# Order of work in a two-block transformer kernel: MLA's fill and keys, neighbourhood scores, weight splits

## The reference

```python
def first_block(x, ...):                       # two layers
    h = rms_norm(x, g_mix[l])
    c_q, c_kv, k_r, qkv_b, qkv_c, gate_logits = split(h @ w_in[l])
    y_a = mla_mixer(c_q, c_kv, k_r, ...)       # 8 heads, latent queries, keys and values, full softmax
    y_b = dilated_mixer(q_b, k_b, v_b)         # 3 groups of 4 heads (dilation 1, 4, 16), banded
    y_c = neighbourhood_mixer(q_c, k_c, v_c, rpb[l])   # 8 heads, 8 x 16 window on a grid, bias
    merged = sum(sigmoid(gate_n) * (y_n @ w_pn[l]) for n in "abc")
    x = x + merged @ w_o[l]
    x = x + (silu(h2 @ w1[l]) * (h2 @ w3[l])) @ w2[l]

def second_block(x, ...):
    x = x + retention_mixer(rms_norm_2(x), ...)    # 4 heads of 256, rope, chunks of 128, decay
    x = x + swiglu_ffn(rms_norm_2(x), ...)
    x = x + rglru_mixer(rms_norm_2(x), ...)        # gelu branch * RG-LRU(conv4(u)), width 1536
    x = x + swiglu_ffn(rms_norm_2(x), ...)
```

## Time and profile before

| | |
|---|---|
| runs | 3466.03 us in the median (3464.95 to 3467.26) |
| the profiled execution | 3467.91 us, its span 3466.1 us |
| mean granted clock | 0.988 of full |
| TensorE matmul (PE) | busy 3376.0 us, 97% |
| VectorE (DVE) | busy 1796.0 us, 52% |
| ScalarE (ACT) | busy 1321.6 us, 38% |
| GpSimd (POOL) | busy 600.6 us, 17% |
| DMA | 86 GB/s in the mean, 25.5% of 16 engines |
| chain that ended last | PE 89%, DVE 6%, ACT 3%, POOL 1%, issue 1% |

### The profile page before, as it was taken

One profiled execution on the slowest core, in us unless ns is written; L12 is line 12 of the kernel. 1 busy time (PEld: TensorE's weight loads), 2 busy tenths in 40 slices (PEclk: granted clock), 3 DMA queues, 4 the chain that ended last, 5 costly groups with the idle time before them and its releaser, 6 DMA issues.

```text
span 3466.1 us, 38536 instructions
## 1 busy us (share of the span) xinstructions
PE 3376.0 (97%) x15644; PEld 2796.1 (81%) x15644; DVE 1796.0 (52%) x2674; ACT 1321.6 (38%) x2018; POOL 600.6 (17%) x518
## 2 busy tenths in 40 slices
PE   8899999999999899999999999999999999999998
PEld 7688778888888777778888878888888887788887
DVE  6755565544437554564444345554544347854433
ACT  4643453333225533543333223332333237843221
POOL 1321022011003320121111001120211014631101
PEclk9999999999999999999999999999999999999999
DMA  3012223222221111222222322222232222223322
GB/s 133 31 56 73 81 78 101 97 97 97 97 97 61 44 61 61 90 82 100 94 97 92 112 69 96 82 79 97 74 97 96 99 67 97 86 73 97 98 97 85
DMA packets 85425, 296.92 MB, mean 86 GB/s; under 512 B 9472, under 2 KB 11776, under 8 KB 85248
## 3 DMA queue, kind: packets, MB, share of 16 engines
q1 hardware_dynamic: 85248, 294.47, 25.5%
HBM read 292.33 MB, written 2.10 MB: 85 GB/s over the span
## 4 chain that ended last, share of the span: by engine, by line
PE 89%; DVE 6%; ACT 3%; issue 1%; POOL 1%; DMA 0%; SPq 0%; POOLq 0%; DVEq 0%; ACTq 0%
PE bank L309 87%; PE bank L312 2%; DVE wl L553 1%; ACT wh L526 1%; DVE small L1209 1%; DVE u_uc L549 1%; DVE m_ptl L553 0%; ACT u_g L529 0%; ACT b_v L526 0%; ACT m_p L529 0%; ACT c_k L526 0%; POOL x L573 0%; DVE m_yf L543 0%; DVE c_kl L553 0%; POOL u_g L573 0%
## 5 line engine op out<-in xcount | busy, mean ns | idle before, releaser
L553 DVE TENSOR_TENSOR wl<-raw,wh 128x1024 fp32r<-128x1024 f32 (+1 forms) x532 | 683.6, 1288 | 888.8 <-ACT wh L526 885.7
L309 PE MATMUL bank<-zh,wh 128*128 128x512 f32 (+1 forms) x2668 | 1043.5, 391 | 30.0 <-ACT b_qk L526 11.1
L309 PE MATMUL bank<-zl,wh 128*128 128x512 f32 (+1 forms) x2668 | 1030.4, 386 | 7.1 <-DVE zl L556 7.0
L309 PE MATMUL bank<-zh,wl 128*128 128x512 f32 (+1 forms) x2668 | 1030.5, 386 | 1.2 <-DVE wl L553 1.2
L526 ACT ACTIVATE wh<-raw 128x1024 fp32r<-128x1024 f32 (+1 forms) x532 | 557.2, 1052 | 566.8 <-PE bank L309 503.0
L309 PEld LDWEIGHTS bank<-zh,wh 128*128 128x128 f32 x2668 | 506.6, 190 | 138.0 <-ACT b_qk L526 14.6
L309 PEld LDWEIGHTS bank<-zh,wl 128*128 128x128 f32 x2668 | 506.1, 190 | 105.5 <-DVE wl L553 3.4
L309 PEld LDWEIGHTS bank<-zl,wh 128*128 128x128 f32 x2668 | 506.1, 190 | 103.9 <-DVE zl L556 9.0
L309 PE MATMUL bank<-f_mh,wh 128*128 128x512 f32 (+1 forms) x748 | 284.7, 381 | 0.0
L309 PE MATMUL bank<-f_mh,wl 128*128 128x512 f32 (+1 forms) x748 | 282.8, 378 | 0.0
L309 PE MATMUL bank<-f_ml,wh 128*128 128x512 f32 (+1 forms) x748 | 281.7, 377 | 0.0
(11 more groups left out here) (340 smaller groups left out, 4648.6 us busy)
## 6 DMA issues: line engine op xcount, KB each, us to landing
raw<-in_wts SPq DMA_DIRECT2D x530, 512.0 KB, 3.3
c_nb<-in_c_bias SPq DMA_DIRECT2D x16, 384.0 KB, 3.1
x<-in_xT SPq DMA_DIRECT2D x8, 256.0 KB, 6.5
out<-x SPq DMA_DIRECT2D x16, 128.0 KB, 1.8
b_mask<-in_b_mask SPq DMA_DIRECT2D x2, 576.0 KB, 3.7
r_d<-in_decay SPq DMA_DIRECT2D x4, 256.0 KB, 2.7
raw<-in_wts SPq DMA_DIRECT2D x2, 256.0 KB, 3.4
m_t<-in_mla_tab SPq DMA_DIRECT2D x2, 256.0 KB, 4.9
```

The lines of the kernel that those rows point to most:

```text
L309: return self.e.matmul(out, l, r, start=start, stop=stop, skip_group_check=inside)
L553: return self.e.tensor_tensor(out, src, b32(hi), ALU.subtract)
```

## The change

No operation is added or taken away, apart from where a split stands in its queue. In eight edits the order changes:

1. The values of the second dilated set (p = 1) take banks 2, 1, 3, 0 in place of 0, 1, 2, 3.
2. MLA's unit 0 has no fill step; all 64 steps of the two layers' fills slide by one, and the last one of a layer goes into unit 31.
3. m_kal leaves DVE's iteration 5 (13, 21) for the end of iteration 4 (12, 20).
4. The projections q2 and k2 of the neighbourhood stand ahead of gate and projection 1 in `FILL_N` (q3 and k3 stay where they are), and pair 2 uses banks 1 and 0 like the others.
5. An iteration's four score products run 128-row, 128-row, 64-row, 64-row, both banks claimed first.
6. Retention: `L.ahead()` ahead of each head's query turn, and after the first.
7. RG-LRU's start: `L.ahead()` between the squares and the gelus on ACT.
8. RG-LRU's rounds: DVE's y_in ahead of the convolution.

The diff:

```diff
--- before.py
+++ after.py
@@ -723,9 +723,12 @@
     return desc
 
 
+BV_BANK = ((0, 1, 2, 3), (2, 1, 3, 0))
+
+
 def tensor_bv(L, l, p, extra={}):
     keys = [("bv", l, p, r) for r in range(4)]
-    L.turned(keys, 3, 8, L.z_tokens(True), bv_desc(l, p), range(4), [("lo",) + n for n in keys], extra)
+    L.turned(keys, 3, 8, L.z_tokens(True), bv_desc(l, p), BV_BANK[p], [("lo",) + n for n in keys], extra)
 
 
 def scalar_bv(L, l, p, rs=range(4)):
@@ -736,8 +739,9 @@
     for r in rs:
         c = m.rcol[:, r:r + 1]
         L.wait_ge("mm", "acc", "bv", l, p, r)
-        L.cp(v0[:, r, :, 0:64], m.bank[r][:, 0:128].rearrange("p (h d) -> p h d", h=2), c)
-        L.cp(v12[:, r, :], m.bank[r][:, 128:384], c).then_inc(*L.tell("hi", "bv", l, p, r))
+        ps = m.bank[BV_BANK[p][r]]
+        L.cp(v0[:, r, :, 0:64], ps[:, 0:128].rearrange("p (h d) -> p h d", h=2), c)
+        L.cp(v12[:, r, :], ps[:, 128:384], c).then_inc(*L.tell("hi", "bv", l, p, r))
 
 
 def vector_bv(L, l, p, rs=range(4)):
@@ -745,7 +749,8 @@
     v0 = m.b_v0[p].rearrange("p (r h d) -> p r h d", r=4, h=2)
     for r in rs:
         L.wait_ge("hi", "bv", l, p, r)
-        L.lo_scaled(v0[:, r, :, 64:128], m.bank[r][:, 0:128].rearrange("p (h d) -> p h d", h=2), m.rcol[:, r:r + 1],
+        ps = m.bank[BV_BANK[p][r]]
+        L.lo_scaled(v0[:, r, :, 64:128], ps[:, 0:128].rearrange("p (h d) -> p h d", h=2), m.rcol[:, r:r + 1],
                     v0[:, r, :, 0:64]).then_inc(*L.tell("lo", "bv", l, p, r))
 
 
@@ -1155,7 +1160,7 @@
             next(q, None)
         if i % 8 == 3 and i < 24:
             tensor_k(L, l, i // 8 + 1)
-        for _ in range((0, 1, 1, 1, 2, 1, 1, 1)[i % 8] if i else 1):
+        for _ in range((0, 1, 1, 1, 2, 1, 1, 1)[i % 8]):
             next(rest, None)
 
     for i in range(32):
@@ -1219,14 +1224,14 @@
             vector_q_turn(L, l, i // 4 + 1)
         if i >= 9 and i % 4 == 1:
             vector_y_add(L, m.m_yt, m.m_yf, (i - 9) // 4, "mla", l)
-        if i % 8 == 5 and i < 28:
-            vector_k_even(L, l, i // 8 + 1)
         if i % 8 == 1 and 1 < i < 32:
             vector_k_odd(L, l, i // 8)
         if i > 8 and i % 8 == 3:
             vector_b_shift(L, ("b", l, 0) + MLA_FILL[i // 8 - 1])
         if i > 8 and i % 8 == 4:
             vector_b_add(L, ("b", l, 0) + MLA_FILL[i // 8 - 1])
+        if i % 8 == 4 and i < 28:
+            vector_k_even(L, l, i // 8 + 1)
         L.ahead()
 
 
@@ -1605,7 +1610,7 @@
 
 
 def c_bank(p, w):
-    return (2, 3)[w] if p == 2 else (1, 0)[w]
+    return (1, 0)[w]
 
 
 def tensor_c(L, l, p, w):
@@ -1671,7 +1676,7 @@
     return [x for n in ns for x in (("g", n), ("p", n))]
 
 
-FILL_N = bb(0, 1) + [("q", 2), ("k", 2)] + bb(2) + [("q", 3), ("k", 3)] + bb(3, 4, 5, 6, 7)
+FILL_N = bb(0) + [("q", 2), ("k", 2)] + bb(1, 2) + [("q", 3), ("k", 3)] + bb(3, 4, 5, 6, 7)
 SLOTS_N = [7] * 4 + [6] * 13 + [4, 2] + [0] * 4
 ENDS_N = ends([{"q": 8, "k": 8, "g": 8, "p": 2}[x] for x, _ in FILL_N], SLOTS_N)
 NV = ("p (c r) -> p r c", dict(r=8)), ("p (r c) -> p r c", dict(r=8))
@@ -1709,18 +1714,18 @@
                              m.c_p[u % 6][:, 128 * x:128 * x + 128])
             t.then_inc(*L.tell("tp", *key, j))
         if it < 16:
-            for i in (2 * it, 2 * it + 1):
-                h, t4 = divmod(i, 4)
-                p, hh = divmod(h, 2)
-                rw = slice(64 * hh, 64 * hh + 64)
-                for what in ("cq", "ck"):
-                    L.wait_ge("lo", what, l, p)
-                L.wait_ge("hi", "ck", l, p)
-                ps = L.claim(4 + i % 2, "mn", *key, i)[:, 0:256]
-                q, k, kl = m.c_q[p % 2][hh], m.c_k[p % 2][hh], m.c_kl[p % 2]
-                qs, ks = slice(128 * t4, 128 * t4 + 128), slice(128 * t4, 128 * t4 + 256)
-                L.mm(ps, q[:, qs], k[:, ks], True, False)
-                L.mm(ps, q[rw, qs], kl[rw, ks], False, True).then_inc(*L.tell("qk", *key, i))
+            h = it // 2
+            p, hh = divmod(h, 2)
+            rw = slice(64 * hh, 64 * hh + 64)
+            q, k, kl = m.c_q[p % 2][hh], m.c_k[p % 2][hh], m.c_kl[p % 2]
+            for what in ("cq", "ck"):
+                L.wait_ge("lo", what, l, p)
+            L.wait_ge("hi", "ck", l, p)
+            two = [(i, L.claim(4 + i % 2, "mn", *key, i)[:, 0:256], 128 * (i % 4)) for i in (2 * it, 2 * it + 1)]
+            for i, ps, o in two:
+                L.mm(ps, q[:, o:o + 128], k[:, o:o + 256], True, False)
+            for i, ps, o in two:
+                L.mm(ps, q[rw, o:o + 128], kl[rw, o:o + 256], False, True).then_inc(*L.tell("qk", *key, i))
         if it >= 4 and it % 2 == 0:
             h = (it - 4) // 2
             Y = L.claim(7, "ev", "y", *key, h)
@@ -2426,7 +2431,10 @@
     L.wait_ge("st", "r1")
     L.cp(m.r_r1, m.bank[4]).then_inc(*L.tell("cp", "r1"))
     for h in range(4):
+        L.ahead()
         scalar_ret_qk(L, "rq", h)
+        if h == 0:
+            L.ahead()
         if h:
             for qt in range(4):
                 scalar_turn(L, h - 1, qt)
@@ -3185,6 +3194,8 @@
         if b:
             vector_scan(L, b - 1)
         lru_reach(L, b, 0)
+        for n in nxt:
+            vector_y_in(L, n)
         if nxt:
             vector_conv(L, nxt)
         lru_reach(L, b, 1)
@@ -3192,8 +3203,6 @@
             vector_hy(L, b - 1)
         for n in nxt:
             vector_us(L, n)
-        for n in nxt:
-            vector_y_in(L, n)
         if b < 6:
             vector_recur_in(L, b)
         lru_reach(L, b, 2)
```

## The result

The changed kernel takes 3417.38 us in the median of four runs (3414.56 to 3420.57), the kernel before 3465.49 in the median of four beside it: a ratio of 0.9863 (0.9846 to 0.9880), 48 us faster. The forecast was 3412, range 3396 to 3440.

The account below looks back on a forecast made before the run. TensorE, busy 97% of the span, was taken as the bound, leaving gaps, slow product switches and half clock to win. Terms 20.6 + 10.8 + 13.8 + 6.2 + 2.8 + 0.6 = 54.8 us gave 3412 us, range 3396 to 3440.

Parts of the forecast that it names:

- RG-LRU's rounds: RG-LRU's middle, y_in ahead of the convolution: u_y waits go, u_hyl starts later; 0.6 us gained.
- MLA: MLA's fill, values' banks and keys' low half: b_qk and m_kal waits go; 20.6 us gained, between 11.6 and 29.6.
- m_ql: MLA: splits that stalls had hidden reappear in DVE's chain, TensorE waits at m_ql, up by 3 to 6 us.
- the forecast's terms without the clock: MLA: 24.2 us of b_qk and m_kal waits gone, 1.4 back for the moved fill step, 5.6 for three splits.
- The term that was off: MLA: of four half-clock stretches behind waits, up to 1.70 us each, only the two behind the values go.
- Neighbourhood: Neighbourhood scores: 10.8 us from products side by side and 13.8 from keys of pair 2 earlier.
- The products' term: Neighbourhood scores: two of four row switches go, 0.386 us an iteration, 12.4 us in 32 iterations.
- c_kl of pair 3: Neighbourhood: the wait for pair 3's keys (1.50 and 1.38 us) grows by about 0.8 in each layer.
- Retention's start: Retention's start: wh queued earlier, wl then decides, about 1.0 us wait stays, half clock goes; 6.2 us, between 2.4 and 6.5.
- RG-LRU's start: RG-LRU's start: wh 1.9 us sooner, about half of a 3.4 us half-clock stretch goes; 2.8 us, between 1.5 and 3.6.
- the bound of 1.5 lost: RG-LRU's rounds, lower end: u_hyl and u_usl start 1.27 us later five times, less 4.9 gained; 1.5 us lost.
- the gain of 4.9: RG-LRU's rounds, upper end: all three u_y waits go, 4.9 us gained.

Follow-up runs that it names:

- the two points of splits alone: The kernel before with only the L.ahead() calls at retention's query turns and between the RG-LRU's squares and gelus (edits 6 and 7): 3458.57 us, ratio 0.9971.
- the first experiment: The kernel before with only the four score products of an iteration reordered to 128, 128, 64, 64 rows (edit 5): 3463.17 us, ratio 0.9980.

## Why the prediction was right

The sum, 54.8 against the 53.4 of the two traces, is closer than its parts: the RG-LRU's rounds came out 3.5 worse than forecast, and stages that the change does not touch, forecast at 0, 3.5 better. That they cancel is luck.

**MLA** (forecast 20.6, measured 22.9). All b_qk and m_kal waits went, as said. DVE's chain took some back, as said, but at another place: not at m_ql (2.8 before and after) but a step ahead, where the next head's query projection claims the bank that DVE's m_qf evicts. DVE and TensorE in layer 0:

```profile
101.76 1.23 DVE L553 TENSOR_TENSOR wl<-raw,wh 128x1024 fp32r<-128x1024 f32 x1 [1.65 <-ACT wh L526]
...
104.16 0.67 DVE L543 TENSOR_TENSOR m_yf<-bank,m_yt 64x512 f32<-64x512 f32 x1
104.76 0.67 DVE L553 TENSOR_TENSOR m_kbl<-m_kf,m_kbh 64x512 fp32r<-64x512 f32 x1
105.36 0.68 DVE L1214 TENSOR_REDUCE small<-bank 128x1 f32<-128x512 f32 x1
...
106.62 0.67 DVE L543 TENSOR_TENSOR m_qf<-bank,m_t 128x512 f32<-128x512 f32 x1
```

```profile
107.34 0.50 PE L309 MATMUL bank<-m_zqh,wh 128*128 128x512 f32 x1 [1.25 <-DVE m_qf L543]
```

The split wl still waits 1.65 us for wh, as in the earlier trace rows, and what stands behind it on DVE without a gap, m_yf, m_kbl, a reduction, m_qf, is late by that; TensorE pays 1.25. All waits of MLA fell from 32.2 us in the two layers to 15.4, that is by 16.8, where the forecast's terms without the clock are 24.2 − 1.4 − 5.6 = 17.2. What was taken back lies elsewhere than forecast, though: nothing at m_ql, 5.4 at m_qf, and 2.1 where TensorE, without the fill step in unit 0, waits for the first softmax (ACT's m_p). The term that was off is the clock: all four stretches at half clock went, not two. How long such stretches are differs between executions of the same code: in the trace with the score products alone, whose MLA is that of before, they take 23.9 us there, 13.7 before.

**Neighbourhood** (24.6, measured 21.1). The products' term was right in sum: TensorE of the changed kernel in iteration 4, to be read beside the earlier trace rows,

```profile
432.26 0.60 PE L312 MATMUL bank<-ident,c_p 128*128 128x128 f32 x4
432.61 0.48 PE L309 MATMUL bank<-c_k,c_q 128*128 128x256 f32 x2
433.02 0.50 PE L309 MATMUL bank<-c_kl,c_q 64*128 64x256 f32 x2
433.45 0.50 PE L309 MATMUL bank<-c_pth,c_v 128*128 128x256 f32 x2
```

has 0.41, 0.43 and 0.84 in all. Its parts were not as said: the second of two equal products follows in 0.20 (behind the transposes) or 0.22 (behind a change of rows), not 0.12, and a change itself takes 0.21, not 0.31. The Trainium skill, TensorEngine Tiling (Array Packing), Key Properties, says that a change of tiling mode drains TensorE; that a change of rows costs 0.20 us here agrees with it. c_kl of pair 3 did not grow (2.9 to 3.0). The terms that were off: c_ptl, c_qf and the evictions of the scores took 2.7 us that the sum did not have, and the stretch at half clock that pair 3's wait of 1.50 has in layer 0, 3.4 us before, is 6.8 us long now (from 483.51), so that the two stages hold 6.8 us of it, not 3.4.

**Retention's start** (6.2, measured 5.7). wl decided, as said; DVE's split and what GpSimd ran beside it:

```profile
2004.40 2.05 DVE L553 TENSOR_TENSOR wl<-raw,wh 128x1024 fp32r<-128x1024 f32 x1
```

```profile
2004.08 3.52 POOL L573 TENSOR_TENSOR r_g<-r_g 128x512 f32<-128x512 f32 x2
```

It took 2.05 us in place of 1.22, so TensorE waits 1.5 for it, not 1.0; the half clock went as said. The split started while the first r_g was running on GpSimd and ended 1.08 us behind that one's end. It is so in the whole trace: of the 530 splits of this shape 475 take 1.20 to 1.24 us, and each of the other 55 (up to 2.33) starts while a GpSimd instruction is running and ends 1.07 to 1.09 us behind that one's end; in the trace of before it is 475 and 55 as well. The Trainium skill, GPSIMD Engine Reference, Specifications, has GpSimd's interfaces to SBUF shared with VectorE, with contention when a VectorE instruction has two inputs in SBUF; the trace agrees (raw and wh both lie there).

**RG-LRU's start** (2.8, measured 3.1). The wait for wh fell from 3.36 to 1.36, as said; the one for wl behind it rose from 0.53 to 0.75, and the half clock behind them stayed. The rest is a stretch of half clock behind an earlier wait, 6.83 us before and 3.4 now. With the two points of splits alone it is the other way round: the 6.83 stay, and the stretch behind wh goes. So the sum is right in part by chance.

**RG-LRU's rounds** (0.6 gained, measured 2.9 lost). This step failed. The prediction saw the mechanism (DVE full, u_hyl behind y_in) and set the 4.9 us of u_y's waits against it as a gain; the run without edit 8 shows that taking them away gains nothing. The 4.9 us come back: 3.4 at u_hyl (2.0 before, 5.4 now) and 1.9 in three new waits for wl, which DVE now also reaches later. The longest of these:

```profile
2927.75 0.50 PE L309 MATMUL bank<-zh,wl 128*128 128x512 f32 x1 [0.98 <-DVE wl L553]
```

DVE, TensorE's wait for u_hyl and the window round it:

```profile
2942.68 4.49 DVE L553 TENSOR_TENSOR wl<-raw,wh 128x1024 fp32r<-128x1024 f32 x2
2947.09 1.27 DVE L543 TENSOR_TENSOR u_y<-bank,rrow 128x512 f32<-128x512 f32 x2
2948.29 4.05 DVE L549 SCALAR_TENSOR_TENSOR u_uc<-u_pad,cols,u_uc 128x512 f32<-128x512 f32 x6
2952.26 1.28 DVE L553 TENSOR_TENSOR u_hyl<-u_h,u_hyh 128x512 fp32r<-128x512 f32 x2
```

```profile
2953.00 0.80 PE L309 MATMUL bank<-u_hyh,wh 128*128 128x512 f32 x1 [5.44 <-DVE u_hyl L553]
```

```profile
2951.34:2958.17 6.83, 5.17 (x12) 4.12 (x13) 6.83 (x11) 4.70 (x7) 2.86 (x1) 0.50 0.02 2
```

y_in at 2947.09 stands ahead of the convolution and u_hyl; TensorE waits 5.4 us for u_hyl in one piece, 2.0 before, and round the end of that long wait it is at half clock for 6.83 us, which the three short u_y waits had not caused. TensorE was busy 5.17 us of these, so they cost about 2.6; with the 0.4 by which the waits grew that is the loss (2.9 up to the table's end of the stage, 3.4 up to the end of the stretch). All six traces with y_in ahead have such a stretch there, and neither of the two with y_in put back. So the step that failed is the bound of 1.5 lost, which left the clock out, and the gain of 4.9 put against it. What makes DVE late is in part GpSimd: the two splits in the first row take 4.49 us in place of some 2.4; both began while a GpSimd instruction was running.

**Elsewhere** (3.5 gained, forecast 0). Stretches at half clock in stages that the change does not touch are there in one execution and not in the other: one of 3.4 us at 1220.40 before, with no wait of TensorE in the 8 us ahead of it, has no counterpart after, but the trace with the banks of the values put back has it, behind the same products. In the whole trace TensorE ran 75 us at half clock before, without the last stretch at the span's end, and 41 after. It was busy 70.5 us of the 75 and 38.0 of the 41; at half pace the difference is some 16 of the 26.4 us by which its busy time fell, and the products' 12.5 are enough for the rest. By this estimate nearly a third of the 53.4 came from the clock.

## What to carry to other kernels

A wait that is removed is worth its length only up to the engine that fills the next one: read which engine has no idle time in that stage (here DVE in the RG-LRU, whose busy time holds its waits for GpSimd) before moving anything ahead in its queue, since an eviction moved ahead there moves everything behind it back. A long wait can cost a stretch of half clock on top of its length, so several short waits can be cheaper than one of the same sum. Where matmuls of different row counts alternate, put equal ones side by side. One shape for all of them gained more here, but added a term to the scores.

## What the runs showed of the hardware

A change between 128-row and 64-row products costs 0.20 us, spread over two products (0.31 each if every product changes, 0.12 if none does). Four 128-row products one after another follow in 0.20, 0.12, 0.12 and 0.12 us, each with new weights whose load has a row of 0.19 us of its own, so a weight load into rows that a running product uses is hidden there. In the changed kernel's trace 67 of DVE's 530 splits start while a GpSimd instruction is running. 55 of them take longer than the others and end 1.07 to 1.09 us behind that instruction's end, so they wait for the whole of it; the other 12 are not delayed. Executions of one kernel differ by 6 us in the changed kernel's four runs (3414.6, 3414.7, 3420.1 and 3420.6), by 12 in 20 runs of the kernel before, and by 14 in the ten of the first experiment. There the time follows the mean granted clock: 3452 to 3454 us at 0.990 and 0.991, 3461 at 0.987 and 0.989, 3465 to 3466 at 0.985 and 0.986. An estimate from these: a mean clock lower by 0.005 is some 35 us more at half clock (1% of the time), which costs some 17 us. Behind pair 3's wait of 1.50 us in layer 0 the traces have a stretch at half clock of 6.8 us (the changed kernel), of 3.4 (banks put back) or none (y_in put back). Why it comes in one execution and not in another is open.
